# Gate slices and the 1024-row branch from seven products of halves instead of eight

## The reference, cut to what matters

```python
proj = x @ w_in                      # x: 256 x 1024
...
br_a = ha.astype(x.dtype) @ w_br_lru      # ha: 256 x 1024
...
br_b = hb.reshape(B, S, ML_V_W).astype(x.dtype) @ w_br_ml     # hb: 256 x 512
...
br_c = hc.reshape(B, S, GD_V_W).astype(x.dtype) @ w_br_gd     # hc: 256 x 512
gates = jax.nn.sigmoid(gate_pre.astype(f32)).reshape(B, S, N_BRANCH, D_MODEL)
merged = gates[..., 0, :] * br_a + gates[..., 1, :] * br_b + gates[..., 2, :] * br_c
y = merged.astype(x.dtype) @ w_out
x = layer_norm(DN_ALPHA * x + y, ln1_g[l], ln1_b[l])
y = moe_ffn(x, router_w[l], router_b[l], exp_w1[l], exp_b1[l], exp_w2[l], exp_b2[l])
x = layer_norm(DN_ALPHA * x + y, ln2_g[l], ln2_b[l])
```

## Time and profile before

| what | value |
|---|---|
| median of 3 runs | 1303.06 us (1302.61 to 1303.66) |
| the profiled execution, its own time | 1303.49 us |
| span of that profile | 1301.7 us |
| TensorE busy | 1258.4 us, 97% |
| VectorE, ScalarE, GpSimd busy | 334.3, 153.6, 9.4 us |
| bytes moved | 462.99 MB |

### The profile page before, as it was taken

How to read it: one execution, slowest core, us unless ns; L and a number is a source line. 1 busy time by engine, 2 the same in 40 slices (tenths; PEclk the granted TensorE clock), 3 DMA queues, 4 the chain that set the end, 5 groups by cost and what they waited for, 6 DMA issues and landing times.

```text
span 1301.7 us, 17875 instructions
## 1 busy us (share of the span) xinstructions
PE 1258.4 (97%) x7714; PEld 683.0 (52%) x7714; DVE 334.3 (26%) x757; ACT 153.6 (12%) x267; POOL 9.4 (1%) x17
## 2 busy tenths in 40 slices
PE   9999999999999999999999999999898999999896
PEld 8888888888873444344343443434343343434341
DVE  4857561231244121211212111121211112110213
ACT  1441621110021000000000000000000000000001
POOL 0000000000000000000000000000000000000001
PEclk9999999999999999999999999999999999999999
DMA  7645327436899999999999999999999999999995
GB/s 269 193 142 176 107 98 289 180 129 223 310 394 400 421 427 425 414 423 428 427 418 427 427 427 426 427 427 428 425 429 427 425 429 428 428 426 428 430 427 238
DMA packets 51175, 462.99 MB, mean 356 GB/s; under 512 B 11896, under 2 KB 13840, under 8 KB 17072
## 3 DMA queue, kind: packets, MB, share of 16 engines
q1 hardware_dynamic: 45280, 459.85, 85.8%
q10 hardware_dynamic: 5840, 2.32, 0.7%
HBM read 460.68 MB, written 1.47 MB: 355 GB/s over the span
## 4 chain that ended last, share of the span: by engine, by line
PE 69%; DMA 19%; DVE 0%; ACT 0%; POOL 0%; issue 0%; POOLq 0%; SPq 0%; DVEq 0%
PE ps L1083 26%; PE ps L629 13%; DMA mix<-expert_w 10%; PE ps L1101 10%; DMA ring<-expert_w 10%; PE ps L980 4%; PE ps L992 4%; PE ps L1076 3%; PE ps L903 2%; PE ps L640 1%; PE ps L1092 1%; PE ps L730 1%; PE ps L1110 1%; PE ps L856 0%; PE ps L877 0%; PE ps L656 0%
## 5 line engine op out<-in xcount | busy, mean ns | idle before, releaser
L1083 PE MATMUL ps<-ring,mix 128*64 128x512 f32 x1512 | 338.3, 593 | 0.1
L629 PE MATMUL ps<-mix 128*128 128x256 f32 x1248 | 274.1, 381 | 0.0
L629 PEld LDWEIGHTS ps<-mix 128*128 128x128 f32 x1248 | 236.3, 190 | 32.6 <-issue 1.2
L1083 PEld LDWEIGHTS ps<-ring,mix 128*64 128x64 f32 x1512 | 106.8, 137 | 194.4 <-issue 190.0
L1101 PE MATMUL ps<-ring,mix 128*64 128x512 f32 x752 | 170.2, 595 | 19.5 <-DMA ring<-expert_w 19.5
L1083 PE MATMUL ps<-mix 128*64 128x512 f32 x536 | 121.1, 594 | 3.9 <-DMA mix<-expert_w 3.7
L2058 DVE TENSOR_SCALAR mix<-ps 128x512 f32<-128x512 f32 x32 | 22.1, 692 | 370.6 <-PE ps L1083 370.6
L1101 PEld LDWEIGHTS ps<-ring,mix 128*64 128x64 f32 x752 | 53.1, 137 | 120.3 <-issue 97.8
L2067 DVE COPY mix<-ps 128x512 f32<-128x512 f32 x32 | 22.1, 692 | 240.6 <-PE ps L1092 240.6
L1083 PEld LDWEIGHTS ps<-mix 128*64 128x64 f32 x536 | 37.8, 137 | 76.9 <-issue 69.7
L1101 PE MATMUL ps<-mix 128*64 128x512 f32 x272 | 62.3, 595 | 5.0 <-DMA mix<-expert_w 5.0
(11 more groups left out here) (279 smaller groups left out, 701.8 us busy)
## 6 DMA issues: line engine op xcount, KB each, us to landing
ring<-expert_w SPq DMA_DIRECT2D x121, 2048.0 KB, 30.6
mix<-expert_w SPq DMA_DIRECT2D x39, 2048.0 KB, 29.3
mix<-stream_w SPq DMA_DIRECT2D x42, 1024.0 KB, 4.8
ring<-expert_w SPq DMA_DIRECT2D x41, 1024.0 KB, 10.0
mix<-expert_w SPq DMA_DIRECT2D x22, 1024.0 KB, 21.8
mix<-stream_w SPq DMA_DIRECT2D x8, 512.0 KB, 3.7
mix<-first_w SPq DMA_DIRECT2D x4, 512.0 KB, 5.0
mix<-planes ACTq DMA_DIRECT2D x1, 1024.0 KB, 7.2
```

Source lines behind the costliest of these rows:

```text
L629: ins = mm(o[:, m * S:(m + 1) * S], w[:, c, m * P:(m + 1) * P], XT[c] if rhs is None else rhs[:, c, :], start=(m == 0 and c == 0), stop=(c ...
L1083: ins = mm(PS[64 * a:64 * a + 64, bank + g, :], XE[j][:, c, 64 * a:64 * a + 64], w[a][:, g * 512:g * 512 + 512], start=False, stop=(c == K ...
```

## The change: what it does

A product of two matrices, each cut in 2 x 2 blocks, is formed from seven block products instead of eight, with sums of blocks before and after. Here the blocks of a slice are: two halves `m` of its 256 columns by two halves `k` of its 1024 rows (each block 4 pieces of 128 x 128), and for the moving side the two halves `k` of the rows by two halves `t` of the tokens. It is done for the sixteen slices `ga..` and `br0.` (`halved(name)`). In the diff, the first `gate` is ScalarE's and `whole` is VectorE's.

TensorE's `proj_halves` makes seven products of four matmuls each, with 128 tokens moving: 28 matmuls (56 records) in place of 16 (32 records). Four of the products go into a first bank (`name + "a"`), three into a second (`name + "b"`). GpSimd forms the sums of the moving side once for `x` (`XS`, at the start) and once for `LY` (`HAS`, after `ha_ready`), four subtractions of 512 words each, and for each slice four sums of weight blocks (`weight_sums(i)`): two into new tiles, one in place in `WB`, one more new. ScalarE copies the first bank to SBUF, VectorE (`whole`) puts the parts together with four additions, and for a gate ScalarE takes the sigmoid from SBUF. The `TAIL` transfer is issued when br03 is done, because its place is used by `HAS`. Some semaphores are merged (`khat`, `kb_ready`, `qb_ready` into `heads`, and others) without another order.

```diff
+def halved(name):
+    return name[:2] == "ga" or name[:3] == "br0"
+def closing(name):
+    return name + "b" if halved(name) else name
...
         for name in names:
-            order.append((name, proj % 4))
-            proj += 1
+            for part in (name + "a", name + "b") if halved(name) else (name,):
+                order.append((part, proj % 4))
+                proj += 1
...
                 elif n > WBUFS:
-                    full(sp, stream[n - WBUFS][0])
+                    full(sp, closing(stream[n - WBUFS][0]))
...
-                if name == "br02":
-                    sp.wait_ge(E("lu_arg"), 1)
+                if name == "ga11":
+                    full(sp, closing("br03"))
                     sp.dma_start(TAIL, expert_w[FAR2[0] * PB + FAR2[1] // (EC // STEPS), FAR2[1] % (EC // STEPS)]
                                  ).then_inc(E("tail_in"), 16)
...
+            def moving_sums(before, out, b11, b12, b21, b22):
+                for n, (dst, left, right) in enumerate(((out[0], b12, b11), (out[1], b22, out[0]), (out[2], b22, b12),
+                                                        (out[3], b21, out[1]))):
+                    nc_g.tensor_tensor(dst, left, right, ALU.subtract).then_inc(E("moving_sums"), 1)
+                    gp.wait_ge(E("moving_sums"), before + n + 1)
+            def weight_sums(i):
+                name = in_halves[i]
+                n = stream_at[name]
+                gp.wait_ge(E(f"w_in{n % WBUFS}"), stream_value(n))
+                if i >= 2:
+                    full(gp, closing(in_halves[i - 2]))
+                a11, a12, a21, a22 = [WB[n % WBUFS][:, 4 * k:4 * k + 4, m * P:(m + 1) * P]
+                                      for m in range(2) for k in range(2)]
+                s1, s2, s4 = WS[i % 2]
+                for k, (dst, left, right, op) in enumerate(((s1, a21, a22, ALU.add), (s2, s1, a11, ALU.subtract),
+                                                            (a21, a11, a21, ALU.subtract), (s4, a12, s2, ALU.subtract))):
+                    nc_g.tensor_tensor(dst, left, right, op).then_inc(E("weight_sums"), 1)
+                    gp.wait_ge(E("weight_sums"), 4 * i + k + 1)
+            full(gp, "gq0")
+            xq = [FIRST_W[:, 2 * k:2 * k + 2, 0, :, t * P:(t + 1) * P] for k in range(2) for t in range(NT)]
+            moving_sums(0, [v.rearrange("p (a b) n -> p a b n", a=2) for v in XS], *xq)
...
+            gp.wait_ge(E("ha_ready"), 1)
+            moving_sums(4, HAS, *[LY[:, 4 * k:4 * k + 4, t * P:(t + 1) * P] for k in range(2) for t in range(NT)])
+            gp.wait_ge(E("mss"), 2 * NT)
+            for i in range(len(in_halves)):
+                weight_sums(i)
...
+                def product(o, at, lhs, rhs, made=None):
+                    if made:
+                        pe.wait_ge(E("weight_sums"), 4 * i + made)
+                    for c in range(4):
+                        ins = mm(o[:, at * P:(at + 1) * P], lhs[c], rhs[c], start=(at == 0 and c == 0), stop=(c == 3),
+                                 skip_group_check=True)
+                    return ins
+                o = take(name + "a")
+                product(o, 0, a(0, 0), b(0, 0))
+                product(o, 3, four(s2), four(sums[1]), 2)
+                product(o, 1, four(s1), four(sums[0]))
+                done(name + "a", product(o, 2, a(1, 0), four(sums[2]), 3))
+                o = take(name + "b")
+                product(o, 0, a(0, 1), b(1, 0))
+                product(o, 1, four(s4), b(1, 1), 4)
+                done(name + "b", product(o, 2, a(1, 1), four(sums[3])))
...
             def gate(k):
-                full(act, f"ga{gates[k]}")
                 if k >= 4:
-                    moved(act, f"br{gates[k - 4]}")
-                A(SG[k % 4], ps(f"ga{gates[k]}"), ACT.Sigmoid).then_inc(free(f"ga{gates[k]}"), 1)
+                    act.wait_ge(E("gate_used"), k - 3)
+                first_part(f"ga{gates[k]}", SG[k % 4])
+                moved(act, f"ga{gates[k]}b")
+                A(SG[k % 4], SG[k % 4], ACT.Sigmoid).then_inc(E("gate"), 1)
+                if k < 4:
+                    if k >= 2:
+                        act.wait_ge(E("gate_used"), k - 1)
+                    first_part(f"br{gates[k]}", MT[k % 2])
...
+            def whole(name, dst):
+                three = dst.rearrange("p (q n) -> p q n", q=4)
+                dve.wait_ge(E("part_copied"), in_halves.index(name) + 1)
+                step(tt(three[:, 3, :], three[:, 0, :], three[:, 3, :], ALU.add))
+                step(tt(three[:, 1:3, :], three[:, 1:3, :], three[:, 3:4, :].to_broadcast([P, 2, P]), ALU.add))
+                tt(three[:, 3, :], three[:, 1, :], ps(name + "a")[:, 2 * P:3 * P], ALU.add
+                   ).then_inc(free(name + "a"), 1)
+                moved(dve, name + "a")
+                full(dve, name + "b")
+                tt(dst[:, 0:3 * P], dst[:, 0:3 * P], ps(name + "b")[:, 0:3 * P], ALU.add).then_inc(free(name + "b"), 1)
+                moved(dve, name + "b")
```

More of the change, by code:

```diff
@@ L222, in layer_kernel @@
     stream_at = {name: n for n, (name, _, _) in enumerate(stream)}
+    in_halves = [name for name, _, _ in stream if halved(name)]
     def stream_value(n):
@@ L489, in _ @@
                 sp.dma_start(X1[:, t, :], x[0, t * P:(t + 1) * P, :]).then_inc(E("x_rows_in"), 16)
-            full(sp, "ga23")
+            full(sp, closing("ga23"))
             load_steps(5, 0, 5)
@@ L621, in weights, with proj_halves @@
                 return WB[n % WBUFS]
+            def proj_halves(name, rhs, sums):
+                w = weights(name)
+                i = in_halves.index(name)
+                s1, s2, s4 = WS[i % 2]
+                a = lambda m, k: [w[:, 4 * k + c, m * P:(m + 1) * P] for c in range(4)]
+                b = lambda k, t: [rhs[4 * k + c][:, t * P:(t + 1) * P] for c in range(4)]
+                four = lambda v: [v[:, c, :] for c in range(4)]
+                def product(o, at, lhs, rhs, made=None):
[14 more added lines that the diff above has]
+                done(name + "b", product(o, 2, a(1, 1), four(sums[3])))
             def proj(name, rhs=None, nk=KD):
+                if halved(name):
+                    if rhs is None:
+                        return proj_halves(name, XT, XS)
+                    return proj_halves(name, [rhs[:, c, :] for c in range(nk)], HAS)
                 w = weights(name)
@@ L708, in _ @@
             proj("ly1")
-            for name, R, ready in (("at", KB, "kb_ready"), ("pt", QB, "qb_ready")):
-                pe.wait_ge(E(ready), 1)
+            for name, R, ready in (("at", KB, 2), ("pt", QB, 3)):
+                pe.wait_ge(E("heads"), ready)
                 for t in range(NT):
@@ L829, in _ @@
                             done(f"w{c}", ins)
+            pe.wait_ge(E("moving_sums"), 4)
             fill(5)
@@ L1400, in _ @@
             act.wait_ge(E("ha_ready"), 1)
-            gate(0)
             for t in range(NT):
@@ L1409, in _ @@
                           ).then_inc(free(f"w{t}"), 1)
-            for k in range(1, 4):
+            for k in range(4):
                 gate(k)
@@ L1822, in _, with gate @@
             branch = [f"{n}{d}" for n in range(3) for d in range(4)]
+            def whole(name, dst):
[9 more added lines that the diff above has]
+                moved(dve, name + "b")
+            def gate(k):
+                whole(f"ga{branch[k]}", SG[k % 4])
             def merge(k):
                 d = k % 4
-                full(dve, f"br{branch[k]}")
-                moved(dve, f"ga{branch[k]}")
                 m2 = MG[:, 2 * d:2 * d + 2, :].rearrange("p c s -> p (c s)")
-                tt(MT[k % 2] if k >= 4 else m2, ps(f"br{branch[k]}"), SG[k % 4], ALU.mult
-                   ).then_inc(free(f"br{branch[k]}"), 1)
-                moved(dve, f"br{branch[k]}")
+                if k < 4:
+                    whole(f"br{branch[k]}", MT[k % 2])
+                    dve.wait_ge(E("gate"), k + 1)
+                    step(tt(m2, MT[k % 2], SG[k % 4], ALU.mult))
+                else:
+                    full(dve, f"br{branch[k]}")
+                    dve.wait_ge(E("gate"), k + 1)
+                    tt(MT[k % 2], ps(f"br{branch[k]}"), SG[k % 4], ALU.mult).then_inc(free(f"br{branch[k]}"), 1)
+                    moved(dve, f"br{branch[k]}")
+                dve.sem_inc(E("gate_used"), 1)
                 if k >= 4:
@@ L1877, in _ @@
                 moved(dve, f"u{t}")
+            gate(0)
             merge(0)
@@ L1887, in _ @@
                        ).then_inc(free(f"ws{c}{k}"), 1)
+                gate(c + 1)
                 if c < NC - 1:
@@ L1903, in _ @@
             o_squares(1)
+            gate(5)
             merge(5)
@@ L1906, in _ @@
             o_scale(1)
+            gate(6)
             merge(6)
@@ L1909, in _ @@
             dve.sem_inc(E("hc_ready"), 1)
-            for k in range(7, 12):
+            gate(7)
+            merge(7)
+            gate(8)
```

(3 more changed lines are left out.)

45 lines of the change are left out of this document (27 added, 18 removed).

## The result

The changed kernel takes 1293.13 us (median of 4 runs, 1292.72 to 1294.08), the kernel before in the same session 1303.36 us (1302.61 to 1303.75): a ratio of 0.9925, 95% interval 0.9912 to 0.9937, 10.2 us less. The forecast was 1292.0 us within 1289.5 to 1299.5.

A forecast was written before the change was run, and what follows sets the result against it. TensorE was taken to bound the first stage, whose end starts the saturated transfers that bound the end. 1303.5 us less 11.4 on TensorE, other terms 0, is 1292.1; 0.4 lower for the median, given as 1292, range 1289.5 to 1299.5.

The forecast's parts named there:

- What bounds the kernel: Whole kernel: TensorE bounds the first stage, whose end starts the saturated transfers; ending d earlier shortens the kernel by d.
- the gain is swallowed: Rival, loads after 350 us: late by a backlog, not by TensorE, so the end stays at 1303.5 us; chance 0.06.
- One sign: Sign of being right, end of the first stage: ga23 done near 337 us, then the same profile 11 us earlier.
- The change on TensorE: Sixteen gate and branch-0 slices: 56 records at 110.6 ns, 6.19 us a slice instead of 6.91, 11.4 us saved.
- The lower bound of 107.9 ns: Best case in the sixteen slices: a record takes exactly half a wide one, 6.04 us a slice, 13.8 us saved.
- the loads' pace: Rival, the slices' records: 116.5 ns or a little more, 6.1 us saved, some 1297.4 us; chance 0.14.
- GpSimd: Sums beside TensorE's slices: 1.30 us an operation, 5.2 us a slice, all hidden, cost 0.
- The threshold of 2.1 us an operation: GpSimd's sums in branch 0: from this length on, a pair of slices is as long as in the kernel before.
- Some sums come late: Rival, a few slices: weights land behind a 2 MB transfer, TensorE waits one or two microseconds, 1294 to 1302; chance 0.08.
- the first of the signs of being wrong: In the changed slices: idle time of TensorE before a product of sums, with GpSimd as releaser.
- VectorE and ScalarE: Additions and copies after the products: `whole` 1.56 us a slice, 25 us over the run, all hidden, cost 0.
- The sum: Whole kernel: 1303.5 - 11.4 = 1292.1 us, the median 0.4 us lower at 1291.7, given as 1292.

The follow-up runs named there:

- gp6: The changed kernel with GpSimd's first sum of each slice made three times, six operations a slice instead of four: 1302.33 us, one run.
- after_again: The changed kernel unaltered, timed again in a later session beside a version with the place-3 transfer issued behind ga23's weights: 1293.18 us, ratio 0.9926.
- split_only: The kernel before, with each wide matmul of the sixteen slices made as two of 128 tokens, all eight block products, no sums: 1306.46 us, ratio 1.0028.
- weights64: The changed kernel with only the first 64 of 128 output channels in each product of halves: 1292.56 us, one run.
- gates_only: The changed kernel with seven products for the twelve gate slices alone, the four branch-0 slices as in the kernel before: 1296.53 us, ratio 0.9950.
- weights64_cols96: The changed kernel with only 64 of 128 output channels and 96 of 128 tokens in each product of halves: 1271.73 us, one run.
- gp8: The changed kernel with GpSimd's first sum of each slice made five times, eight operations a slice instead of four: 1340.65 us, one run.

## Why the prediction was right, point by point

**What bounds the kernel.** Right in both steps. TensorE is the bound in the first stage (slices back to back in the chain), and every saturated transfer hangs on its end: the rest of the kernel keeps its length within 0.8 us over a range of 68 us of the stage. The rival "the gain is swallowed" is thereby excluded. One sign was put at the wrong slice: 337 us is where the stage was to end, and it ended at 337.8; ga23 itself was done at 331.1, some 11 us sooner than before.

**The change on TensorE** was mis-sized by one nanosecond: 111.6 ns a record and 6.25 us a slice instead of 110.6 and 6.19. The saving is 16 x (6.906 - 6.25) = 10.5 us and not 11.4. The step that failed was the scaling: the 111.5 ns of the earlier trace rows were measured at 129 columns, and I took 1/129 of them off because I held the tokens for what sets the pace. The weights do, and they are 128 wide in both, so the row should have been taken as it stood. (By its tokens alone, 128 x 0.833 + 2.5, a record would take 109.2 ns.) The lower bound of 107.9 ns couldn't be reached even with lighter weights. The rival "the loads' pace" had the right mechanism with the wrong number; 116.5 ns came from the lengths of the loads, 111.6 from the distance of the starts. Against the narrow tile the Trainium skill (TensorE: Matmul & The Clock Gate, Back-to-back issue gap) has a step of about 81 ns for pairs of 128 columns against some 56 alone. In this case it is 111.6 ns against 109.2 with half the weights: the direction agrees, that a load paces a narrow record, and the size doesn't for float32.

**GpSimd.** 1.27 us an operation where it runs alone, 1.60 where it is held, against 1.30; 5.4 to 5.6 us a slice. Hidden except at ga23. The nearness to the bound is now known: at six operations a slice nothing measurable is left of the gain (1302.33 against 1303.81 us, one run each), and at eight the kernel is slower than before. The threshold of 2.1 us an operation, 8.4 us a slice, was too generous: gp6 with about 8.1 us a slice gives 1302.3, since a wait costs its idle time, a quarter of a microsecond more, and at times the clock.

**Some sums come late.** This rival, given 0.08, happened in the small: 0.7 us once, which is also the first of the signs of being wrong that the prediction named. Its working named 4.9 us behind a 2 MB transfer and 3.1 us to spare. What was overlooked is the rule for place 3, which puts such a transfer ahead of just the tightest slice's weights: they were issued at 314.22 us, and the first sum started 8.6 us later. By the stage the wait costs 0.9 us where it is 0.67 long, and 0.8 where it is 0.57 (after_again).

**VectorE and ScalarE.** Right that both stay hidden, and the durations were right where an input comes from PSUM (the 128-word additions of `whole` 0.286 to 0.289 us, the 384-word ones 0.554, forecast 0.29 and 0.56). The holding is larger than allowed, about 1.0 us for an operation instead of 0.4 to 0.7, and meets multiplications by a scalar, of which I had thought nothing. It was hidden because VectorE is busy 60.6 of 141 us beside TensorE. The Trainium skill (SBUF — State Buffer, Who interferes with whom) has the later instruction wait whole, and names such multiplications too where they run in a fast mode with both port pairs. The trace agrees: alone they take 68 ns for 128 words more (281 and 349 ns), half of an addition's 1.05 ns a word, and they are held.

**The sum.** 11.4 - 0.9 for the record's pace - 0.9 for the wait is 9.6 us; the stage shows 9.5. TAIL left SP at 256.43 us, 35 us later as said, and neither its move nor the copies show in the sum. That the medians differ by 10.2 leaves 0.7 us, within what the start alone varies from one execution to the next (1.2 us). That much of the nearness of 1293.1 to 1292.0 is luck.

## What to carry to other kernels

Products of halves pay here because the load of 128 columns of weights nearly hides behind 128 tokens: ask first whether the narrower record costs half (split_only, 3.4% more than half), since the whole gain is an eighth of the records. Take the start-to-start distance of a record of the same weight width, and don't scale it by the tokens where the weights set the pace. The sums then need an engine with slack at the tightest slice, counted from the issue of that slice's weights with every transfer ahead of it in the same queue, and a wait of TensorE costs more than its idle time: a quarter of a microsecond more, and twice as much in all where the clock fell behind a wait of 1.91 us.

## What the runs showed of the hardware that I hadn't expected

- A float32 record with 128 columns of weights steps at 111 to 112 ns at 96, 128 or 129 tokens. With 64 columns of weights it steps at 109.2 ns for 128 tokens and 82.5 ns for 96, and a wide record (128 columns, 256 tokens) at 215.8: these three lie on 0.833 ns a token and 2.5 ns a record.
- Neighbouring streams whose weights differ in width cost time at the meeting: in weights64 a branch slice between two such slices takes 3.65 us instead of 3.46, and the slice itself 6.26 where its step makes 6.11. The reason stays open.
- GpSimd's additions hold VectorE's multiplications by a scalar from SBUF to SBUF, 128x256 in 1.42 us instead of 0.35, and `whole`'s additions with an input in PSUM not at all (0.286 to 0.289 us for 128 words, in all sixteen slices).
- A wait of TensorE in a stream of these records costs 0.26 us beyond its idle time, and it can halve the granted clock (1.2 instead of 2.4 GHz) for the 3 to 6 us behind it: it did after waits of 1.91 (gates_only), 2.19 (weights64_cols96), 3.25 (gp6) and, in gp8, 3.39 to 6.25 us, and did not after one of 2.43 (gp8), 1.94 (gp6) or 0.67 (the changed kernel). In gates_only and gp6 that cost 1.7 us each on top of the wait, and the length of the wait alone doesn't tell which way it goes.
